# Two-part, 16-byte piecewise reading of the moving operand in the FFN output products of a three-block transformer kernel

## What is computed

```
def swiglu(x, w_in, w_out):
    a, b = jnp.split(x @ w_in, 2, axis=-1)
    return (jax.nn.silu(a) * b) @ w_out
```

## Time and profile before

| | |
|---|---|
| median of three runs | 1784.22 us |
| the profiled execution, its own time | 1784.11 us |
| its span, first to last instruction | 1781.9 us (2.2 us less than its time) |
| instructions | 31794 |
| TensorE matmul (PE) | busy 1757.3 us, 99%, 12924 matmuls |
| TensorE weight load (PEld) | busy 1625.6 us, 91% |
| VectorE (DVE) | busy 1090.2 us, 61% |
| ScalarE (ACT) | busy 920.6 us, 52% |
| GpSimd (POOL) | busy 36.3 us, 2% |
| read from memory | 322.12 MB, 181 GB/s over the span |
| mean granted TensorE clock | 0.998 of 2.4 GHz |

### The profile page before, as it was taken

How to read it: one execution, slowest core, us unless ns; L and a number is a source line. 1 busy time by engine, 2 the same in 40 slices (tenths; PEclk the granted TensorE clock), 3 DMA queues, 4 the chain that set the end, 5 groups by cost and what they waited for, 6 DMA issues and landing times.

```text
span 1781.9 us, 31794 instructions
## 1 busy us (share of the span) xinstructions
PE 1757.3 (99%) x12924; PEld 1625.6 (91%) x12924; DVE 1090.2 (61%) x1457; ACT 920.6 (52%) x1218; POOL 36.3 (2%) x60
## 2 busy tenths in 40 slices
PE   8999998999999999999999999999999999999998
PEld 8999877999999999898899999999999898989997
DVE  6555776655565566566676555655574657675554
ACT  5444666444454445577755444544464577645443
POOL 0000220000000000000000000000000000000000
PEclk9999999999999999999999999999999999999999
DMA  7555523555555555453355555555555443446552
GB/s 308 201 191 189 186 95 120 216 201 194 205 206 195 192 179 192 182 192 119 135 184 191 189 188 196 199 199 200 191 198 176 178 171 119 152 155 222 192 188 95
DMA packets 46689, 324.34 MB, mean 182 GB/s; under 512 B 5392, under 2 KB 5648, under 8 KB 8464
## 3 DMA queue, kind: packets, MB, share of 16 engines
q1 hardware_dynamic: 44208, 315.81, 49.5%
q10 hardware_dynamic: 2400, 7.38, 1.1%
HBM read 322.12 MB, written 1.05 MB: 181 GB/s over the span
## 4 chain that ended last, share of the span: by engine, by line
PE 95%; ACT 3%; DVE 1%; issue 1%; DMA 0%; DVEq 0%; POOLq 0%; POOL 0%; ACTq 0%
PE work L1525 21%; PE work L1527 20%; PE work L1526 20%; PE acc L1527 8%; PE acc L1526 8%; PE acc L1525 8%; PE work L1579 4%; PE acc L1776 2%; PE acc L1758 1%; PE acc L1768 1%; ACT prob L731 1%; DVE lo L1011 1%; PE work L1626 0%; PE acc L1635 0%; ACT hi L610 0%
## 5 line engine op out<-in xcount | busy, mean ns | idle before, releaser
L1011 DVE TENSOR_TENSOR lo<-raw,hi 128x2048 fp32r<-128x2048 f32 x280 | 641.0, 2291 | 335.7 <-ACT hi L610 335.2
L1525 PE MATMUL work<-xT_hi,hi 128*128 128x256 f32 x2656 | 738.4, 278 | 1.2 <-DVE lo L1011 1.2
L610 ACT ACTIVATE hi<-raw 128x2048 fp32r<-128x2048 f32 x280 | 535.5, 1915 | 385.6 <-PE work L1527 353.5
L1527 PE MATMUL work<-xT_hi,lo 128*128 128x256 f32 x2656 | 734.4, 277 | 0.0
L1526 PE MATMUL work<-xT_lo,hi 128*128 128x256 f32 x2656 | 734.3, 276 | 0.0
L1525 PEld LDWEIGHTS work<-xT_hi,hi 128*128 128x128 f32 x2656 | 498.5, 188 | 10.5 <-issue 5.6
L1526 PEld LDWEIGHTS work<-xT_lo,hi 128*128 128x128 f32 x2656 | 499.3, 188 | 2.5
L1527 PEld LDWEIGHTS work<-xT_hi,lo 128*128 128x128 f32 x2656 | 498.6, 188 | 0.0
L1527 PE MATMUL acc<-hi,hT_lo 128*128 128x512 f32 x480 | 189.1, 394 | 0.0
L1526 PE MATMUL acc<-lo,hT_hi 128*128 128x512 f32 x480 | 188.2, 392 | 0.0
L1525 PE MATMUL acc<-hi,hT_hi 128*128 128x512 f32 x480 | 186.7, 389 | 0.0
(11 more groups left out here) (278 smaller groups left out, 2024.4 us busy)
## 6 DMA issues: line engine op xcount, KB each, us to landing
raw<-stream SPq DMA_DIRECT2D x298, 1024.0 KB, 4.8
mem_in<-mem ACTq DMA_DIRECT2D x3, 1024.0 KB, 6.2
post<-post ACTq DMA_DIRECT2D x6, 512.0 KB, 3.7
x<-x SPq DMA_DIRECT2D x2, 512.0 KB, 4.6
out<-x SPq DMA_DIRECT2D x4, 256.0 KB, 2.1
alibi<-alibi ACTq DMA_DIRECT2D x1, 768.0 KB, 10.3
params<-l_params SPq DMA_DIRECT2D x2, 328.0 KB, 5.5
params<-b_params SPq DMA_DIRECT2D x1, 534.0 KB, 10.0
```

Source lines behind the costliest of these rows:

```text
L610: nc.scalar.activation(hi[:, s, :], raw[:, s, :], ACT.Copy).then_inc(hi_ready, 1)
L1011: nc.vector.tensor_tensor(lo[:, s, :], raw[:, s, :], hi[:, s, :].bitcast(F32), ALU.subtract).then_inc(lo_ready, 1)
L1525: nc.tensor.matmul(dst, a_hi, b_hi, start=start, stop=False)
L1527: return nc.tensor.matmul(dst, a_lo, b_hi, start=False, stop=stop)
```

## The change

The host lays the columns of the FFN output weights down in another order, and the matmuls read them back in the old order. Within each 512 columns the weights are stored in two parts of 256 elements (1 KB): of each 8 columns in turn the first 4 go to the first part and the other 4 to the second. The moving operand is read with three dimensions: 64 groups, in each group 4 elements (16 bytes) of the first part and 4 of the second, whose addresses are 1 KB apart. The output in PSUM is described with the same three dimensions; there they run over 512 consecutive elements. Numbers of instructions, loads, splits, waits and bytes are what they were; the mixers' products are not changed.

```
+                def halves(w):
+
+                    return w.rearrange("p (j g k) -> p g j k", j=2, k=4)
+
                 def out_tile(n, i, h, first=False, final=False):
 
                     s = sec.slot(n)
                     for c in range(2):
                         for f in range(2):
                             w = slice(D * f + 512 * c, D * f + 512 * c + 512)
-                            last = product(acc[:, 2 * i + c, :], h[0][:, f, P * i:P * i + P], h[1][:, f, P * i:P * i + P],
-                                           hi[:, s, w], lo[:, s, w], first and f == 0, final and f == 1)
+                            last = product(acc[:, 2 * i + c, :].rearrange("p (g j k) -> p g j k", j=2, k=4),
+                                           h[0][:, f, P * i:P * i + P], h[1][:, f, P * i:P * i + P],
+                                           halves(hi[:, s, w]), halves(lo[:, s, w]), first and f == 0, final and f == 1)
...
-        outof.append(w_out[CHUNK * j:CHUNK * (j + 1)].reshape(2, P, D).transpose(1, 0, 2).reshape(P, UNIT))
+        t = w_out[CHUNK * j:CHUNK * (j + 1)].reshape(2, P, 2, 64, 2, 4)
+        outof.append(t.transpose(1, 0, 2, 4, 3, 5).reshape(P, UNIT))
```

## The result

The kernel with the change takes 1829.56 us (median of 4 runs, 1829.19 to 1830.02), against 1784.83 us for the kernel before (4 runs, 1783.42 to 1787.31). The ratio is 1.025, with a 95% interval of 1.0238 to 1.0263. The profiled execution took 1830.02 us, 45.9 us more than the 1784.11 us of before; its span is 1827.8 us.

What follows compares the result with a forecast made beforehand. TensorE was taken to bound the kernel, passing on every nanosecond. 1584 edited matmuls winning 5.7 ns each gave 9.0 us, so 1784.1 - 9.0 = 1775.1, forecast 1775.2 us; range 1763 to 1805 us.

Steps and rivals of the forecast that it cites:

- What bounds the kernel: TensorE, busy 99% of the span; a nanosecond on an edited matmul arrives one to one, up to 25 us.
- What costs nothing: Host order, loads, splits, weight loads, waits and queues add no time; PSUM's three dimensions none unless patterns cost by dimensions.
- two walks at half the rate each: Moving read of edited matmuls: memory can't keep up with one full-rate walk, so two should gain; 5.7 ns per matmul.
- relief: Forecast that edited matmuls get faster, to 215.9 to 227.0 ns from 229.2; chance 0.46.
- half-rate rows: Plain float32 matmuls and transposes at two cycles per column, read as losing only 2.6 ns or next to nothing.
- The bounds: Distance between starts of edited matmuls: from 215.9 ns (21.1 us won) to 432 ns (321 us lost).
- middle value: Edited matmul's excess falls to a 256-column matmul's 6.8 ns: 220.1 ns, 14.4 us won.
- weak bound: Edited matmul at twice the 256-column form's low level: 227.0 ns, 3.5 us won.
- Rival A: No change: the number of 16-byte pieces fetched costs, 128 in both orders; 1784.2 us, chance 0.22.
- Rival B: Edited stream slower by phase steps of 4.3 ns, one to three: 1791 to 1804.6 us, chance 0.14.
- Rival C: Edited read loses a gap per broken run, runs assumed 64 bytes: 268.7 ns, 1847 us, chance 0.14.
- wrong in another way: Unedited input side moves to its 117.8 ns level as the output side's phase changes: 27 us lost, held unlikely.

Runs made afterwards that it cites:

- e2: The change with pieces of 256 bytes instead of 16, parts still 1 KB apart: output-side matmul 229.0 ns, total 1783.6 us.
- e6: The change with pieces of 8 bytes instead of 16, each 16-byte line visited twice: output-side matmul 340.1 ns, total 1958.7 us.
- e5: The change with pieces of 64 bytes instead of 16, parts still 1 KB apart: output-side matmul 240.0 ns, total 1824.5 us.
- e7: The change with its two walks replaced by one walk of 16-byte pieces with gaps of 16 bytes: output-side matmul 232.6 ns, total 1816.4 us.
- e1: The change with pieces of 32 bytes instead of 16, parts still 1 KB apart: output-side matmul 243.3 ns, total 1816.5 us.
- e10: The change with the second part 1056 bytes behind the first instead of 1 KB: output-side matmul 244.0 ns, total 1806.4 us.
- e13: The change with the second part 1152 bytes behind the first instead of 1 KB: output-side matmul 243.2 ns, total 1806.1 us.
- e14: The change with the second part 1088 bytes behind the first instead of 1 KB: output-side matmul 240.9 ns, total 1803.2 us.
- e16: The change applied to only 6 of the 24 matmuls of an output side: average 236.1 ns per output-side matmul, total 1796.2 us.
- e17: The change with its two walks replaced by one descending walk of 16-byte pieces over the same 2 KB: output-side matmul 233.6 ns, total 1788.9 us.
- e18: The change with pieces of 256 bytes and the base of each read moved by 128 bytes: output-side matmul 232.9 ns, total 1790.6 us.

## Why the prediction was wrong, point by point

**What bounds the kernel** was right. TensorE passes every nanosecond on: the 46.3 us counted on PE's timeline are the 45.9 us of the total.

**What costs nothing** was right. Loads and splits show no change, and e2 has PSUM described with three dimensions, as the change has, at no cost. An LDWEIGHTS record of the output side lasts 188 ns before and 189 to 190 after.

**The failed step** is the sentence that the new order "makes it two walks at half the rate each". I had put 13.2 of the 15.8 ns down to reading 4 bytes in each cycle from one place, took them to go away at half the data rate, and took that for a limit of a place, which two places would share. The runs show the opposite: two places in turn cost more than one, at every distance tried and at every piece length under 256 bytes (229 ns in a row; in 16-byte pieces 233 to 236 for a single walk and 241 to 251 for two). The forecast of -5.7 ns for a matmul was +21.4. The evidence for relief was the half-rate rows. At best these have fewer bytes per cycle; they don't have two places. No row of before had two, so the sign had no row behind it. Nor do show a half rate by themselves. Their eight records are four matmuls of the program, two heads by two token tiles: `scores` (L1758) counts its semaphore up twice in four matmuls, and the trace has 64 counts on 256 records. So a plain float32 matmul stands there as two records and takes 0.43 us for 256 columns. A record that spends 512 cycles on 256 columns can have read them once at half the rate, or twice at the full one; in the second case full-rate reading cost 2.6 ns there, and not 15.8. No run tells which.

**The bounds** held on the slow side (432 ns) and failed on the fast side: no read order tried was faster, on average over an output side, than the one in a row. The middle value had a slip of its own: it counted the 6.8 ns that a 256-column matmul loses once, for two parts. Twice it is 227.0 ns, the weak bound, so by its own argument the sum should have been 2.2 x 1584 = 3.5 us won, and not 9.0.

**Rival A** fell, and the rule beside it with it. The Trainium skill ("Advanced Engine Details and Errata", "SBUF Cachelines") has each 16-byte line hide its fetch when it is hit at least twice. The change hits every line four times in a row and loses 21.4 ns; two hits at a time (e6) lose 111 ns. The measurement decides against the rule for this read: hits in a line are not enough where the next line is far away. **Rival B** had the right kind of thing for the input side but too small a price for the edited matmuls: 21.4 ns is five of its steps of 4.3 ns, where three were its end. **Rival C** had the right side, that jumps cost more than they save, with the wrong size and a mechanism that e5 refutes: 64-byte pieces would have been free, and 16-byte pieces would cost 39.5 ns, not 21.4. The measured 1830 us lies between B's and C's times, where I had put nothing.

**The input side** was the "wrong in another way" of the text: its 117.8 ns level, priced at 27 us and held for unlikely. It came in every second chunk and took 12.3 us, a quarter of the loss. The argument against it, that it returns to 113.5 ns after each output side, was drawn from output sides at 229 ns. After other output sides it does not return: in e5 (240.0 ns) and e7 (232.6 ns) nearly all input sides ran at 117.8, in the change and in e1 (243.3 ns) every second one, in e10, e13, e14, e16, e17 and e18 next to none. It is not the pace by itself that decides: e14 at 240.9, e13 at 243.2 and e18 at 232.9 ns stand right beside e5, e1 and e7, and stayed low.

**What stays open.** Why reading far pieces in turn costs: the low bits of the distance carry about 9 ns of it, and the remaining 12 or so have no cause that a run here shows. Whether it is the turns or the far jumps is not separated, and whether four walks are worse for their number or for their distance isn't either. Banks with a period of 256 bytes would explain the equality of 512, 1024 and 1280 bytes, but not the 14.3 ns that stay at 1152. Why a 256-byte piece is free at one base and costs 3.9 ns at another is open as well, and so is what puts the input side on one level or the other.

## What to carry to other kernels

Give the moving operand of an fp32r stream like this one its columns in a row. If it must be read from two places, pieces of 256 bytes were free at the base tried and cost 3.9 ns at a base 128 bytes on, while 16-byte pieces cost 9%: take long pieces, and measure. Before reordering a read to relieve a limit, find a row that has the new access, not one that only has less of the old. Check that such a row is what it looks like: a record may be a part of a matmul. And where one stream's pace changes, look at its unedited neighbours: they may change level too.

## What the runs showed of the hardware that was not expected

- Reading 16-byte pieces in turn costs 21.4 ns per 512 columns for two places 512 or 1024 bytes apart, and 40 for four places 512 bytes apart; a descending read costs 4.7 ns, a read with gaps 3.7 (16 bytes) or 7.4 (48 bytes).
- The places may be 512, 1024 or 1280 bytes apart without a nanosecond's difference in the average (250.3), but 32 to 128 bytes more than 1 KB make it 241 to 244.
- The same unedited matmuls of 256 columns run at 113.5 or 117.8 ns for a whole input side, with the granted clock at 1.00 in both. Which level it is changed with the read of the output side before them, but does not follow from its pace alone.
- A plain float32 matmul is two pairs of weight load and matmul in the trace, 0.216 us each for 256 columns; an fp32r matmul is one, at 113.5 ns.
- 8-byte pieces take 340 ns, 49% over the read in a row.
- No variant beat the kernel before. The nearest, e2, gave 1783.6 us against 1784.4 in its session, which is no difference that this measurement can tell.
